# Seven products of block sums instead of eight in the down projections of two SwiGLU stages

## The reference

```
x = x + 0.5 * rmsnorm((silu(h @ Wg) * (h @ Wu)) @ Wdown, post_g)    # h = rmsnorm(x, pre_g)
# h: 256x1024, Wg and Wu: 1024x2816, Wdown: 2816x1024
```

## Time and profile before

| | |
|---|---|
| median of three runs | 1080.41 us |
| profiled execution, its time | 1081.31 us |
| its span, first to last instruction | 1079.4 us |
| TensorE matmuls busy | 1068.7 us, 99% of the span |
| VectorE busy | 789.1 us, 73% |
| ScalarE busy | 608.5 us, 56% |

### The profile page before, as it was taken

One profiled execution on the slowest core, in us unless ns is written; L12 is line 12 of the kernel. 1 busy time (PEld: TensorE's weight loads), 2 busy tenths in 40 slices (PEclk: granted clock), 3 DMA queues, 4 the chain that ended last, 5 costly groups with the idle time before them and its releaser, 6 DMA issues.

```text
span 1079.4 us, 21082 instructions
## 1 busy us (share of the span) xinstructions
PE 1068.7 (99%) x8534; PEld 1009.7 (94%) x8534; DVE 789.1 (73%) x1125; ACT 608.5 (56%) x905; POOL 0.2 (0%) x4
## 2 busy tenths in 40 slices
PE   9999999999999999999999999999999999999999
PEld 7999999999989999999999998999999799999898
DVE  5665556989979777778778555775655887997884
ACT  5544444678586545878445556444444575655471
POOL 0000000000000000000000000000000000000000
PEclk9999999999999999999999999999999999999999
DMA  9866556465543454444546533465556355542251
GB/s 343 292 213 211 176 182 209 151 221 174 179 154 121 152 181 157 157 164 149 208 166 244 196 106 130 147 230 198 188 182 212 119 177 200 191 157 95 102 196 39
DMA packets 29297, 190.71 MB, mean 177 GB/s; under 512 B 3656, under 2 KB 4521, under 8 KB 7466
## 3 DMA queue, kind: packets, MB, share of 16 engines
q1 hardware_dynamic: 26480, 182.53, 48.6%
q10 hardware_dynamic: 2746, 7.16, 1.9%
HBM read 188.62 MB, written 1.05 MB: 176 GB/s over the span
## 4 chain that ended last, share of the span: by engine, by line
PE 87%; DVE 9%; ACT 2%; issue 1%; DMA 1%; SPq 0%; DVEq 0%; ACTq 0%
PE bank L526 15%; PE bank L528 15%; PE bank L527 15%; PE bank L538 10%; PE bank L539 10%; PE bank L540 10%; DVE sb_w_lo L2098 3%; PE bank L625 2%; PE bank L761 1%; DVE sb_ssd_conv L2409 1%; DMA sb_w_raw<-in_w 1%; PE bank L709 1%; PE bank L886 1%; ACT sb_w_hi L1371 1%; PE bank L1048 1%
## 5 line engine op out<-in xcount | busy, mean ns | idle before, releaser
L2098 DVE TENSOR_TENSOR sb_w_lo<-sb_w_raw,sb_w_hi 128x2048 fp32r<-128x2048 f32 x169 | 386.4, 2289 | 118.9 <-ACT sb_w_hi L1371 118.5
L1371 ACT ACTIVATE sb_w_hi<-sb_w_raw 128x2048 fp32r<-128x2048 f32 x169 | 322.9, 1911 | 33.0 <-PE bank L528 29.2
L526 PE MATMUL bank<-sb_hT_hi,sb_w_hi 128*128 128x256 f32 (+1 forms) x816 | 225.7, 277 | 0.0
L528 PE MATMUL bank<-sb_hT_hi,sb_w_lo 128*128 128x256 f32 (+1 forms) x816 | 225.7, 277 | 0.0
L527 PE MATMUL bank<-sb_hT_lo,sb_w_hi 128*128 128x256 f32 (+1 forms) x816 | 225.6, 276 | 0.0
L538 PE MATMUL bank<-sb_hT_hi,sb_w_hi 128*128 128x256 f32 (+2 forms) x744 | 213.1, 286 | 0.2 <-DVE sb_hT_lo L2175 0.2
L539 PE MATMUL bank<-sb_hT_lo,sb_w_hi 128*128 128x256 f32 (+2 forms) x744 | 206.2, 277 | 0.0
L540 PE MATMUL bank<-sb_hT_hi,sb_w_lo 128*128 128x256 f32 x744 | 205.9, 277 | 0.0
L526 PEld LDWEIGHTS bank<-sb_hT_hi,sb_w_hi 128*128 128x128 f32 (+1 forms) x816 | 152.7, 187 | 0.0
L528 PEld LDWEIGHTS bank<-sb_hT_hi,sb_w_lo 128*128 128x128 f32 (+1 forms) x816 | 152.6, 187 | 0.0
L527 PEld LDWEIGHTS bank<-sb_hT_lo,sb_w_hi 128*128 128x128 f32 (+1 forms) x816 | 152.6, 187 | 0.0
(11 more groups left out here) (516 smaller groups left out, 2077.9 us busy)
## 6 DMA issues: line engine op xcount, KB each, us to landing
sb_w_raw<-in_w SPq DMA_DIRECT2D x169, 1024.0 KB, 4.9
sb_w_raw<-in_w SPq DMA_DIRECT2D x4, 512.0 KB, 7.8
sb_hT<-in_xT SPq DMA_DIRECT2D x2, 512.0 KB, 5.3
sb_x<-in_x SPq DMA_DIRECT2D x2, 512.0 KB, 11.8
sb_mem_xn<-in_mem ACTq DMA_DIRECT2D x1, 1024.0 KB, 7.1
sb_mem_T<-in_memT ACTq DMA_DIRECT2D x1, 1024.0 KB, 10.4
sb_post_g<-in_ffn_post_g ACTq DMA_DIRECT2D x2, 512.0 KB, 5.7
sb_decay<-in_c_decay ACTq DMA_DIRECT2D x1, 768.0 KB, 5.3
```

The lines of the kernel that those rows point to most:

```text
L526: pe.matmul(o, a_hi, b_hi, start=first, stop=False)
L528: return pe.matmul(o, a_lo, b_hi, start=False, stop=last)
L1371: act.activation(w_hi[b % STAGES][:], w_raw[b % RING][:], ACT.Copy).then_inc(w_hi_in, 1)
L2098: tt(w_lo[b % STAGES][:], w_raw[b % RING][:], f32(w_hi[b % STAGES][:]), ALU.subtract).then_inc(w_lo_in, 1)
```

## The change

A down block's work for a pair of tiles is a product of tokens (2 halves) by 256 hidden (2 tiles) with 256 hidden by 1024 columns. For c = 1 to 8 of both stages the columns 512 to 1023 are now done as before (`plain_half`), and the columns 0 to 511 are taken as a 2x2 by 2x2 product of blocks of 128x128 and 128x256, for which seven products of sums of blocks are taken in place of eight. The sums of weight blocks (three, `mix_raw`, and one written back in place into the raw buffer) are made by VectorE in `mix_block`, and split in `mix_hi` and `mix_lo`; the sums of hidden tiles (four, `sum_raw`) in `first_sum` and `other_sums`, and split in `sum_hi` and `sum_lo`. The seven products gather over the eight pairs in the halves of banks 3, 4, 5 and 6 and are combined once, in `join`, behind pair 8. Pairs 0, 9 and 10 are done plainly. Banks 5 and 6 are opened with a matmul of zeros (`open_banks`, in the middle of up block 3; for ffn1's bank 6 at the kernel's start). The loop has seven turns in place of eight, up blocks use two banks, and pair 10 takes its four parts in another order. The host reorders the columns of the sixteen blocks.

```diff
-PAIR_TURNS = PAIRS - 3
+PAIR_TURNS = PAIRS - 4
+MIXED_PAIRS = PAIRS - 3
+MIXED_OF = {down_at(n, c): MIXED_PAIRS * (n - 1) + c - 1 for n in (1, 2) for c in range(1, PAIRS - 2)}
...
+                    tile_in(c, 0, turn)
+                    plain_half(banks[7], 0, top)
+                    tile_in(c, 1, turn)
+                    plain_half(banks[7], 1, top)
+                    of_tile(5, 0, 0, top, hi, lo, b11, False)
+                    of_tile(3, 0, 1, top, hi, lo, b21, False)
+                    of_tile(4, 0, 1, low, mix_hi, mix_lo, u4, True)
+                    pe.wait_ge(S("ffn_sum_lo"), MIXED_PAIRS * (n - 1) + c + turn)
+                    of_sum(3, 1, 3, hi, lo, b22, True)
+                    of_sum(5, 1, 0, mix_hi, mix_lo, u1, True)
+                    of_sum(6, 0, 1, hi, lo, u2, False)
+                    of_sum(6, 1, 2, mix_hi, mix_lo, u3, True)
+                    plain_half(banks[last_bank], 0, low)
+                    last = slice(PLAIN_AT + 512, PLAIN_AT + 1024)
+                    last_product(banks[last_bank], hi[:, last], lo[:, last], parts, all_three).then_inc(block_done, 1)
+                def open_banks():
+                    pe.wait_ge(S("zero_r"), n)
+                    w = w_hi[up_at(n, 3) % STAGES]
+                    for q in range(n):
+                        open_mixed(n, q)
+                        pe.matmul(banks[5 + q][:], zero_r[:], w[:, 0:512], start=True, stop=False)
...
-                down_block(0, 0, *LAST_DOWN[n][0])
-                up_block(3)
+                plain_block(0, *LAST_DOWN[n][0])
+                up_block(3, between=open_banks)
                 with pe.Fori(0, PAIR_TURNS) as turn:
                     up_block(4, turn)
-                    down_block(1, turn, *LAST_DOWN[n][1])
+                    mixed_block(1, turn, *LAST_DOWN[n][1])
                     up_block(5, turn)
+                up_block(FF_TILES - 4)
+                mixed_block(PAIRS - 3, 0, *LAST_DOWN[n][1])
+                up_block(FF_TILES - 3)
...
+                if b in MIXED_OF:                                         # round_block, ScalarE
+                    act.wait_ge(S("ffn_mixed"), MIXED_OF[b] + 1 + turn)
+                    act.activation(w_hi[b % STAGES][:], w_raw[b % RING][:], ACT.Copy)
+                    act.activation(mix_hi[:], mix_raw[:], ACT.Copy).then_inc(w_hi_in, 1)
+                def sums_high(c, turn=0):
+                    act.wait_ge(S("ffn_sum"), MIXED_PAIRS * (n - 1) + c + turn)
+                    act.activation(sum_hi[:], sum_raw[:], ACT.Copy).then_inc(S("ffn_sum_hi"), 1)
...
+                if b in MIXED_OF:                                         # low_block, VectorE
+                    ins = tt(mix_lo[:], mix_raw[:], f32(mix_hi[:]), ALU.subtract)
+            def mix_block(b, turn=0):
+                dve.wait_ge(w_landed[b % RING], 16 * (b // RING + 1 + turn))
+                tt(mix_raw[:, 0:512], quarter(0, 2), quarter(1, 3), ALU.add).then_inc(S("ffn_mixing"), 1)
+                dve.wait_ge(S("ffn_mixing"), 2 * p + 1 + 2 * turn)
+                tt(quarter(1, 2), mix_raw[:, 0:256], quarter(2, 3), ALU.add).then_inc(S("ffn_mixing"), 1)
+                dve.wait_ge(S("ffn_mixing"), 2 * p + 2 + 2 * turn)
+                tt(mix_raw[:, 512:768], quarter(1, 2), quarter(3, 4), ALU.add).then_inc(S("ffn_mixed"), 1)
...
+                    tt(sum_raw[:, 2, :], even[:, 0:P], even[:, P:SEQ], ALU.subtract).then_inc(S("ffn_summing"), 1)
...
+                    tt(sum_raw[:, 1, :], sum_raw[:, 2, :], odd[:, P:SEQ], ALU.add)
+                    tt(sum_raw[:, 0, :], even[:, P:SEQ], odd[:, P:SEQ], ALU.subtract).then_inc(S("ffn_summing"), 1)
+                    tt(sum_raw[:, 3, :], odd[:, 0:P], sum_raw[:, 1, :], ALU.subtract).then_inc(S("ffn_sum"), 1)
...
+                    tt(sum_lo[:], sum_raw[:], f32(sum_hi[:]), ALU.subtract).then_inc(S("ffn_sum_lo"), 1)
...
+                def join():
+                    link(tt(w, o[:, 0:256], y[:, 0, 0:256], ALU.subtract))
+                    link(tt(y[:, 0, 256:512], w, p5, ALU.add))
+                    tt(y[:, 1, 0:256], o[:, 256:512], w, ALU.subtract)
+                    read(tt(y[:, 1, 256:512], y[:, 0, 256:512], o[:, 256:512], ALU.subtract), f"mixed{n}.1")
+                    for t in range(TOK):
+                        key = f"mixed{n}.{2 + t}"
+                        read(tt(y[:, t, :], full(dve, key)[:], y[:, t, :], ALU.add), key)
...
+                    mixed = 2 <= j < 2 * PAIRS - 4                         # hidden_tile, VectorE
+                        if j % 2:
+                            other_sums(j // 2, turn)                       # ahead of ffn_lo
+                    for b in behind:
+                        if b in MIXED_OF:
+                            mix_block(b, turn)                             # ahead of `between`
+                    if mixed:
+                        (sums_low if j % 2 else first_sum)(j // 2, turn)   # behind ffn_lo
...
+                hidden_tile(FF_TILES - 4, [b], [b + 1], 0, [lambda: None, join])
+                hidden_tile(FF_TILES - 3, [], [b + 2])
```

More of the change, by code:

```diff
@@ L733, in up_block @@
                         ready = second_ready if b == SPLIT_FROM else None if j else norm_done(norm)
-                        feature_block(f"up{n}.{j}", b, 2, hT_hi, hT_lo, ready=ready, between=between)
+                        feature_block(f"up{n}.{j}", b, 2, hT_hi, hT_lo, bank=up_bank(j), ready=ready, between=between)
                         return
                     pe.wait_ge(w_lo_in, b + 1 - SPLIT_FROM + TURN * turn)
-                    o = claim_turns([f"up{n}.{j + 2 * i}" for i in range(PAIR_TURNS)], b % 3, b, turn)
+                    o = claim_turns([f"up{n}.{j + 2 * i}" for i in range(PAIR_TURNS)], up_bank(j), b, turn)
@@ L739, in up_block, with tile_in, last_product @@
                     feature_products(o, b, 2, hT_hi, hT_lo, key=f"up{n}.{j}").then_inc(block_done, 1)
-                def down_block(c, turn=0, parts=(512,), all_three=False):
+                def tile_in(c, k, turn):
+                    pe.wait_ge(S("ffn_lo"), FF_TILES * (n - 1) + 2 * c + 1 + k + 2 * turn)
+                def last_product(o, w_hi, w_lo, parts, all_three):
+                    t = slice(P, SEQ)
+                    for m, (a, w) in enumerate(((f["hi"], w_hi), (f["hi"], w_lo), (f["lo"], w_hi))):
+                        at = 0
+                        for width in parts if all_three or m == 2 else (512,):
+                            mm = pe.matmul(o[:, at:at + width], a[:, 1, t], w[:, at:at + width], start=False, stop=False)
+                            at += width
+                    return mm
@@ new lines, in open_banks, with plain_block @@
+                def open_banks():
[4 more added lines that the diff above has]
+                        pe.matmul(banks[5 + q][:], zero_r[:], w[:, 0:512], start=True, stop=False)
+                def plain_block(c, parts=(512,), all_three=False):
+                    b = down_at(n, c)
+                    first, last = c == 0, c == PAIRS - 1
+                    pe.wait_ge(w_lo_in, b + 1 - SPLIT_FROM)
+                    hi, lo = halves(b, 2, D)
+                    if first:
+                        for i in range(4):
+                            claim(f"down{n}.{i}" if i % 2 else f"mixed{n}.{2 + i // 2}", down_banks[i],
+                                  None if i == 1 else down_at(n, PAIRS - 1 if i == 3 else PAIRS - 3))
+                    elif not last:
+                        for i in (0, 2):
+                            claim(f"down{n}.{i}", down_banks[i])
@@ L764, in down_block @@
+                            if k and i == 3 and not last:
+                                mm = last_product(o, hi[:, 1, h], lo[:, 1, h], parts, all_three)
+                                continue
+                            mm = product(o[:], f["hi"][:, k, t], f["lo"][:, k, t], hi[:, k, h], lo[:, k, h],
+                                         k == 0 and (first or not last and i % 2 == 0), last and k == 1)
+                            if last and k == 1 and i < 3:
                                 ends(mm, f"down{n}.{i}")
@@ L778, in ffn_part @@
                 up_block(FF_TILES - 2)
-                down_block(PAIRS - 2, 0, *LAST_DOWN[n][2])
+                plain_block(PAIRS - 2, *LAST_DOWN[n][2])
                 up_block(FF_TILES - 1)
-                down_block(PAIRS - 1)
+                plain_block(PAIRS - 1)
             pe.wait_ge(S("zeros"), 1)
             stay_warm(zeros[:, 0:P], zeros[:], 1)
+            open_mixed(1, 1)
+            pe.matmul(banks[6][:], zeros[:, 0:P], zeros[:], start=True, stop=False)
             ffn_part(1, 0)
             for i in range(4):
-                feature_block(f"kv{i}", FIRST["xa_k"] + i, 2, mem_hi, mem_lo, ready=None if i else mem_ready)
+                feature_block(f"kv{i}", FIRST["xa_k"] + i, 2, mem_hi, mem_lo, bank=(0, 1, 0, 2)[i],
+                              ready=None if i else mem_ready)
```

(5 more changed lines are left out.)

135 lines of the change are left out of this document (104 added, 31 removed).

## The result

The changed kernel takes 1084.62 us (median of six runs, 1083.92 to 1086.11), the kernel before, beside it on the same chip, 1080.93 us: a ratio of 1.0036, 95% interval 1.0023 to 1.0049. It is slower, by 3.7 us; the forecast's sum was 4.0 us and its time 1084.7 us. The profiled execution took 1084.47 us, its span is 1082.7 us, 3.3 us longer than before.

The account below looks back on a forecast made before the run. TensorE, with matmuls in flight for 99% of the span, was taken as the bound. The terms -3.8 + 0.9 + 0.2 + 2.5 + 1.4 + 1.2 + 1.8 + 0.5 - 0.7 = +4.0 us gave 1084.7 us, range 1077.5 to 1090.5.

Parts of the forecast that it names:

- products, 16 blocks: In 16 mixed down blocks, 21 matmuls of 256 columns replace 12 of 512, all at the slow rhythm: -3.8 us.
- opening, rhythm behind it: In up block 3, one matmul of zeros in ffn1, two in ffn2, with some slower matmuls behind: +0.9 us.
- kernel's start with `zero_r`: At the kernel's start, early zeros may raise TensorE's clock, -0.7 us; making `zero_r` on VectorE costs +0.2 us.
- stall ahead of ffn1's up 6: Ahead of ffn1's up block 6, VectorE's additions make the low weight part late and TensorE waits: +2.5 us.
- ffn2's start, up 2, 4, 5: At ffn2's start, VectorE's additions and a bank wait delay up blocks 2, 4 and 5: +1.4 us.
- last down blocks: In each stage's last down block, VectorE's lag and `join` stall TensorE: +1.2 us in ffn1, +1.8 in ffn2.
- behind them, ffn1 and ffn2: Behind the last down blocks, adding banks makes x later: 0.1 us uncovered in ffn1, 0.4 more in ffn2.
- rival 2: In the loop, the slow matmul rhythm stays in the up blocks: +6.9 us, about 1089.5 us; chance 0.17.
- VectorE's turn: One loop turn takes VectorE 15.7 us without idle time against TensorE's 16.1; a lag shrinks 0.35 us a turn.
- Rival 3: VectorE bounds the loop, its turn taking 16.5 us in place of 15.7: about 1091 us; chance 0.08.
- rival 1: VectorE's additions hide in gaps, ffn1's up block 6 starting within 0.5 us of before: -1.8 to -3.4 us; chance 0.2.
- Rival 4: Over the whole kernel, saving and stalls of some 4 us cancel: 1080.4 us within 2.2; chance 0.15.

Follow-up runs that it names:

- e1: The kernel before with one more matmul of zeros at its start and nothing else of the change: 1080.83 us, ratio 1.0001.
- e10: e8's kernel with the last of the seven products taken twice, so eight products per mixed block, output not the reference's: 1084.09 us.
- e2: The changed kernel with mem's squares on ScalarE and their root in an idle gap of VectorE: 1082.26 us, ratio 1.0037.
- e3: The changed kernel with the joining of the seven products left out, output not the reference's: 1083.06 us in one run.
- e5: The changed kernel with side work of tiles 20 and 21 in VectorE's idle times of tiles 18 and 19, transpose of mem's root moved: 1085.65 us.
- e7: The changed kernel with the moves of e2 and e5, half of mem's low part at tile 20, ffn2's fold difference later: 1082.82 us, ratio 1.0024.
- e8: e7's kernel with the transpose of mem's root behind up block 18 and ffn2's fold begun one step earlier: 1078.02 us, ratio 0.9979.

## Why the prediction was right

Measured terms are differences of TensorE's positions between the two profiled executions; in both the column of the granted clock shows 1.00 throughout.

| step | forecast | measured |
|---|---|---|
| products, 16 blocks | -3.8 | -4.4 (16 x 0.274, the turn 16.387 to 16.113) |
| opening, rhythm behind it | +0.9 | +1.0 |
| kernel's start with `zero_r` | -0.5 | -1.1 in this trace, none to be told in the time (e1) |
| stall ahead of ffn1's up 6 | +2.5 | +2.35 |
| ffn2's start, up 2, 4, 5 | +1.4 | +0.7 (0.18, 0.37, 0.18) |
| slow rhythm in ffn2's up 0 to 2 and 4 | none | +0.8 |
| last down blocks | +1.2, +1.8 | +1.27, +1.39 |
| behind them, ffn1 and ffn2 | +0.1, +0.4 | +0.85, +0.2 |
| sum | +4.0 | +3.1 (span +3.3, medians +3.7) |

*Products.* 113.3 and 227 ns held. Of the 21 matmuls of 256 columns 9 are slow (119 to 120 ns) and 12 fast, where I had taken all for slow, so the saving is 0.6 us larger. The loop's up blocks behind them are fast, 113.5 ns in the mean: rival 2 is out. One of my signs of being wrong, up blocks at 118 ns, did come outside the loop, in ffn1's up blocks 3 (second half) and 4 and ffn2's 0 to 2 and 4; it costs the 0.8 us of the table and 0.3 of the opening's 1.0. e10 shows that the length counts in full.

*VectorE's turn.* Forecast 6.94 + 8.8 = 15.7 us; in ffn1 it is 82.91 - 76.02 = 6.89 and 91.86 - 82.91 = 8.95, together 15.84. The low part of the odd up blocks 7 to 19 comes 0.28, 0.55, 0.82, 1.09, 1.35, 1.62 and 1.89 us ahead of TensorE in successive turns (80.70 + 2.29 = 82.99 before 83.54 is the second): a lag is worked off at 0.27 us a turn, where I said 0.35. In ffn2 the turn is 15.76 and the lag goes at 0.35. "Without idle time" was wrong in the words: VectorE idles 2.8 us of the turn, for ScalarE, part of which the sum held as the wait for the silu. The turn is a chain through both engines, so VectorE's busy time does not give it. Rival 3 is out.

*Start of ffn1.* Up block 6 begins at 56.64, 1.5 us later than before, so rival 1, which needed 0.5, is out; e2 shows that the chain through mem's root, with the additions ahead of it, was the cause. *Ends.* The join made these stalls: without it they go (e3), and with 2.5 us of the work behind it moved into idle times ahead of it they go as well (e5).

*What was mis-sized.* "In ffn1 the key blocks cover that but for 0.1" failed: it is 0.85 (1.05 ahead of kv2, where the kernel before had 0.20). I followed x to the transposes and not to the next weight block; kv2's low part stands on VectorE behind x. From the first step behind down block 10 to that low part it was 7.78 us (193.63 to 201.41 in the trace before), and with the banks added it is 203.13 - 194.57 = 8.56. e3 shows that the join has no part in it, e7 and e8 that 1.2 us less on VectorE behind tile 21 take it back to 0.22 and 0.25. ffn2's start was over-sized by half, and the slow rhythm in up blocks 0 to 2 and 4 there was not in the sum at all; the two nearly cancel. The kernel's start was worth 0.6 us more in this trace than forecast, but e1 finds no such gain in the time. So the total owes something to luck, and that 1084.7 stands 0.1 us beside the measured 1084.62 is luck altogether: the traces differ by 3.2 us, the medians by 3.7. The large terms, the products, the stall of up block 6 and the two of the join, came within 0.6 us each by their own mechanisms.

Rival 4, that saving and stalls cancel, failed with the interval of the ratio, which excludes 1.

## What to carry to other kernels

Here a saving on the engine that bounds a steady loop was kept in full in the loop (e10), and what it cost on the next engine was paid at the loop's ends, where side work shares that engine. Price each low-slack place by name before the change, and fill the engine's idle times ahead of it with side work, rather than take work off it: here that turned +3.7 us into -2.4. Follow a delayed result to everything that stands behind it in the same engine's queue, and a moved step to the last reader of the bank that it takes.
